# Attention probabilities and the retention output turned by VectorE in 32x32 blocks and through device memory instead of by TensorE

## The chip, the core and the metric

The kernel runs on one core of a Trainium2 chip. TensorE (PE) multiplies, ScalarE (ACT) and VectorE (DVE) do elementwise work, GpSimd (POOL) some small steps, and SyncE (SP) issues most DMAs, which move data between device memory and the core's buffers on 16 DMA engines. The metric is the time of one execution on the device, in microseconds (us); smaller is better.

## What is computed

A decoder of two layers over 256 tokens, width 1024, all in float32. In each layer a mixer of attention (8 heads, three dilated groups) and retention (4 heads), then a gated convolution MLP:

```python
def token_mixer(x, positions, w_in, w_attn_proj, w_ret_proj, ret_gn_g, ret_gn_b, w_out):
    proj = x @ w_in
    attn_qkv, ret_q, ret_k, ret_v, ret_g, gate_a, gate_r = jnp.split(proj, offsets, axis=-1)
    ...
        o, l = dilated_window_attention(attn_qkv[:, :, gi, 0], attn_qkv[:, :, gi, 1], attn_qkv[:, :, gi, 2], window, dilation)
    ...
    ret = chunkwise_retention(...)
    ret = head_group_norm(ret, ret_gn_g, ret_gn_b)
    ret = (jax.nn.silu(ret_g.astype(jnp.float32)) * ret).astype(x.dtype)
    merged = jax.nn.sigmoid(gate_a) * (attn @ w_attn_proj) + jax.nn.sigmoid(gate_r) * (ret @ w_ret_proj)
    return merged @ w_out

def reference(...):
    for i in range(DEPTH):
        mix = token_mixer(...)
        x = layer_norm(DN_ALPHA * x + mix, ln1_g[i], ln1_b[i])
        ple = jax.nn.sigmoid(x @ w_ple_gate[i]) * (p[i] @ w_ple_proj[i])
        x = layer_norm(DN_ALPHA * x + conv_ffn(x, w_up[i], conv_w[i], conv_b[i], w_down[i]) + ple, ln2_g[i], ln2_b[i])
    return x
```

## The kernel before

Weights stream through a ring of three slots in chunks of 1 MB (2048 floats on each of 128 partitions). SP loads a chunk into `raw` once the chunk three before it has been used up by DVE (`load` waits on `lo_ready`). ACT copies it, rounded, to `w_hi` (`to_hi`), DVE takes the difference as `w_lo` (`to_lo`), and PE multiplies with both parts. In chunk c's step ACT and DVE make chunk c + 2. Every engine runs its own program in a fixed order, and semaphores tie them; nothing is scheduled by a planner.

A layer's mixer has four passes (j = 0 to 3) of 15 chunks; pass j makes two attention heads and one retention head. `both_parts` is a chunk of one kind of product (5.6 us on PE), `two_chunks` multiplies two chunks together (chunks 1 and 2, and 11 and 12), `by_token` is chunk 0. The head work stands between the chunks (`behind(c)` on PE): the scores of head 0 behind chunk 9, the retention scores behind 12, the scores of head 1 and the retention products behind 13. DVE masks the scores, takes the maximum, and normalises the probabilities in `prob` (`normalise(0)` in chunk 11's step, `normalise(1)` in chunk 14's), then scales the retention output into `ret_y`. All these live in the tensor `scratch`, the name that the profile shows.

The products with the values need the probabilities with the keys on the partitions, so TensorE transposes them: `transpose_prob` turns the 8 blocks of 128x128 of one head into the banks `acc`, and ACT copies them to `probT` (`copy_probT`). Head 0's stand behind chunk 12, head 1's behind chunk 0 of the next pass, together with the 8 of the retention output (`transpose_ret`), which ACT's `finish_ret` takes with scale and bias to `ret_t`; DVE multiplies by the gate, and both make the parts `ret_hi` and `ret_lo`. `attend` follows behind chunks 1 and 2. After the last pass a merge begins with two gate chunks, the product with `ret` in two halves, attention in between, and the product with `attn`; there the transposes stand behind the gate chunks. In all, 192 transposes: 24 for each of 8 passes.

SP's only work is the DMA queue, in program order: a wait there holds everything behind it.

Of the kernel before, what the change touches and what calls it, by code (L numbers as in the profile page):

```python
# [22 lines left out]
P = 128  # L23
# [9 lines left out]
RV = 512  # L33
# [64 lines left out]
def program(nc, x, xT, positions, w_in, w_attn_proj, w_ret_proj, w_out, w_up, w_down,  # L98
            w_ple_gate, ple_operands, ln_rows, feature_params, constants, out):
    ctx = ExitStack()  # L100
    with ctx:
# [47 lines left out]
        probT = view(0, (2, TT, 512))  # L149
        prob = view(2048, (TT, 512))  # L150
        decayed = view(3456, (384,))
        ret_y = view(3840, (TT, RV))
        silu = view(4864, (4, SEQ))
# [3 lines left out]
        ret_t = view(6912, (4, SEQ))  # L157
        qk = view(7936, (6, 2, SEQ))
# [62 lines left out]
        probT_done, probT_copied, pv_done = sem("probT_done"), sem("probT_copied"), sem("pv_done")  # L221
# [8 lines left out]
        ret_yT_done, ret_affine, ret_gated = sem("ret_yT_done"), sem("ret_affine"), sem("ret_gated")  # L230
# [45 lines left out]
        def _(sp):  # L276
# [20 lines left out]

            def mixer_loads(l, j, c_from):
# [11 lines left out]
                for c in range(c_from, C_MIX):  # L310
                    load(l, l * C_LAYER + j * C_MIX, c, part(w_in, l, 0, KT, cols[c], CH))

# [4 lines left out]
            for l in range(DEPTH):  # L317
# [27 lines left out]
                load(l, g, 1, part(w_in, l, 0, KT, GR0, CH))  # L345
                load(l, g, 2, part(w_ret_proj, l, 0, KT, 0, CH))
                load(l, g, 3, part(w_ret_proj, l, KT, KT, 0, CH))
                load(l, g, 4, part(w_attn_proj, l, 0, KT, 0, CH))
                for j in range(NJ - 2):
# [49 lines left out]
        def _(act):  # L399
# [26 lines left out]
            def copy_probT(a, n):  # L426
                act.wait_ge(probT_done, n)
                for t in range(TT):
                    ins = nc.scalar.activation(probT[:, a, t, :], acc[t][:, :], ACT.Copy)
                ins.then_inc(probT_copied, 1)  # L430

            def finish_ret(l, j, done, src):

                act.wait_ge(ret_yT_done, done)
                act.wait_ge(feat_in, 16 * DEPTH)
                for k in range(4):
                    ins = nc.scalar.activation(ret_t[:, k, :], src[k // 2][:, (k % 2) * SEQ:(k % 2 + 1) * SEQ],
# [3 lines left out]
                if j < NJ - 1:  # L441
                    copy_probT(1, done * 2)
# [20 lines left out]
            def mixer(l, j):  # L463
# [15 lines left out]
                def retention_scores():  # L479
                    copy_probT(0, it2 + 1)  # L480
                    act.wait_ge(decayed_ready, it + 1)
                    nc.scalar.activation(decayed_hi, decayed, ACT.Copy).then_inc(decayed_hi_ready, 1)
# [7 lines left out]
                for c in range(C_MIX):  # L490
# [6 lines left out]
                    if j and c == 1:  # L497
                        finish_ret(l, j - 1, it, (acc[2], acc[3]))
# [15 lines left out]
                    if j and c == 0:  # L514
                        gates_silu(l, j)
                    if c == v0:
# [50 lines left out]
            for l in range(DEPTH):  # L567
# [23 lines left out]
                for c in range(5):  # L591
# [4 lines left out]
                    if c == 1:  # L596
                        finish_ret(l, NJ - 1, (l + 1) * NJ, (acc[2], acc[3]))
                        gate_sigmoid(0, 0)
                        gate_low(c0 + 1, 0, 1)
                    if c == 2:  # L600
                        copy_probT(1, (l + 1) * NJ * 2)
# [165 lines left out]
        def _(dve):  # L767
# [153 lines left out]
            def mixer(l, j):  # L921
# [60 lines left out]

                def decay_scores():
# [21 lines left out]
                for c in range(C_MIX):  # L1005
# [6 lines left out]
                    if j and c == 1:  # L1012
                        finish_ret(j - 1, it)
                    if j and c == 3:
                        finish_attn(j - 1, it)
                    if c in (rv, rv + 1):
# [7 lines left out]
                        else:  # L1024
                            nc.vector.tensor_tensor(rv_lo[:, t, :], bank[bank_of(c)][:, :], rv_hi[:, t, :].bitcast(F32),
                                                    ALU.subtract).then_inc(bank_read[bank_of(c)], 1)
                    if one_by_one and c == 3:
# [12 lines left out]
                    if c == 11:  # L1040
                        normalise(0)
                    if c == 12:
                        decay_scores()
                    if c == 14:
                        normalise(1)
                        dve.wait_ge(gn_rstd, it + 1)
# [3 lines left out]
                                                ALU.subtract, ALU.mult).then_inc(ret_y_ready, 1)  # L1050
                        high_part(14, silu[:, 2:4, :], 1.0)
# [747 lines left out]
```

## Time and profile before

| | before |
|---|---|
| time, median of 3 runs | 1482.85 us (1482.59 to 1483.01) |
| span of the profiled execution | 1480.9 us |
| PE busy | 1471.0 us, 99% |
| DVE busy | 1017.0 us, 69% |
| ACT busy | 784.8 us, 53% |
| DMA | 266.86 MB, mean 180 GB/s |

The profiled execution is one run; its span goes from the first to the last instruction, and the 2.0 us between it and the median lie outside. An engine's timeline row gives the start, the length, the line, the operation and its tensors, and in brackets how long the engine was idle before it and what ended that. In the chain that ended last, followed back from the end, PE has 96%.

### The profile page before, as it was taken

How to read it: one execution, taken by the hardware profiler on the slowest of the kernel's cores; microseconds unless marked ns; L12 is line 12 of the kernel's file. 1: busy time of each engine (PE TensorE's matmuls, PEld its weight loads, DVE VectorE, ACT ScalarE, POOL GpSimd, SP SyncE). 2: the span in 40 equal slices, each digit the busy share in tenths (PEclk: the TensorE clock that was granted, in tenths of full speed). 3: DMA queues.
4: the chain of work that ended last, by engine and by line, in shares of the span. 5: the costliest groups of instructions: out<-in, count | busy, mean ns of one | idle time of the engine just before them, and what ended most of it. 6: DMA issues, size and time to landing. Idle time of an engine off the chain costs nothing.

```text
span 1480.9 us, 20354 instructions
## 1 busy us (share of the span) xinstructions
PE 1471.0 (99%) x8369; PEld 1292.9 (87%) x8369; DVE 1017.0 (69%) x1165; ACT 784.8 (53%) x845; POOL 46.0 (3%) x30
## 2 busy tenths in 40 slices
PE   9999999999999999999999999999999999999998
PEld 8888898888888888888888888888888888888886
DVE  6765665756755688777866657667566556887777
ACT  5564554554744456566544545546446444566562
POOL 0000000000000020000010000000000000100000
PEclk9999999999999999999999999999999999999999
DMA  9745446455456565655555555454545565665560
GB/s 315 236 145 170 155 158 199 143 170 168 147 188 214 181 213 178 207 197 199 175 173 167 168 171 165 150 194 147 170 149 187 177 205 177 202 221 177 181 237 36
DMA packets 232621, 266.86 MB, mean 180 GB/s; under 512 B 4320, under 2 KB 222944, under 8 KB 231904
## 3 DMA queue, kind: packets, MB, share of 16 engines
q1 hardware_dynamic: 231728, 264.96, 53.8%
q8 instruction: 58, 0.95, 0.3%
q10 hardware_dynamic: 816, 0.79, 0.2%
q14 instruction: 19, 0.16, 0.0%
HBM read 264.68 MB, written 1.05 MB: 179 GB/s over the span
## 4 chain that ended last, share of the span: by engine, by line
PE 96%; DMA 1%; DVE 1%; ACT 1%; issue 0%; SPq 0%; DVEq 0%; ACTq 0%
PE bank L1337 39%; PE bank L1342 20%; PE bank L1323 7%; PE bank L1325 6%; PE bank L1324 6%; PE acc L1323 4%; PE acc L1324 4%; PE acc L1325 4%; DMA raw<-w_in 1%; PE acc L1510 1%; PE acc L1487 1%; PE acc L1465 1%; PE acc L1483 1%; PE acc L1472 0%; PE acc L1530 0%; PE acc L1452 0%
## 5 line engine op out<-in xcount | busy, mean ns | idle before, releaser
L775 DVE TENSOR_TENSOR w_lo<-raw,w_hi 128x2048 fp32r<-128x2048 f32 x234 | 535.6, 2289 | 262.8 <-ACT w_hi L408 262.5
L408 ACT ACTIVATE w_hi<-raw 128x2048 fp32r<-128x2048 f32 x241 | 459.5, 1908 | 149.8 <-PE bank L1325 80.1
L1337 PE MATMUL bank<-xT_both,w_hi 128*128 128x512 f32 x2208 | 528.3, 391 | 0.2 <-DVE scratch L932 0.2
L1337 PEld LDWEIGHTS bank<-xT_both,w_hi 128*128 128x128 f32 x2208 | 407.5, 188 | 81.3 <-DVE scratch L932 0.4
L1342 PEld LDWEIGHTS bank<-xT_both,w_lo 128*128 128x128 f32 x2208 | 283.1, 191 | 10.8
L1342 PE MATMUL bank<-xT_both,w_lo 128*128 128x256 f32 x2208 | 286.4, 283 | 0.0
L528 ACT ACTIVATE scratch<-bank 128x512 f32<-128x512 f32 x80 | 47.8, 598 | 229.6 <-PE bank L1342 229.6
L1323 PE MATMUL bank<-w_hi,xT_both 128*128 128x512 f32 (+1 forms) x464 | 162.1, 349 | 0.4 <-DVE xT_both L843 0.3
L1325 PE MATMUL bank<-w_hi,xT_both 128*128 128x512 f32 (+1 forms) x464 | 161.0, 347 | 0.0
L1324 PE MATMUL bank<-w_lo,xT_both 128*128 128x512 f32 (+1 forms) x464 | 160.9, 347 | 0.0
L1185 DVE SCALAR_TENSOR_TENSOR scratch<-scratch,feat 128x256 f32<-128x256 f32 x176 | 77.4, 481 | 33.7 <-ACT scratch L685 28.8
L1323 PEld LDWEIGHTS bank<-w_hi,xT_both 128*128 128x128 f32 x464 | 88.6, 191 | 11.8 <-issue 0.9
L1325 PEld LDWEIGHTS bank<-w_hi,xT_both 128*128 128x128 f32 x464 | 88.6, 191 | 10.8
L1324 PEld LDWEIGHTS bank<-w_lo,xT_both 128*128 128x128 f32 x464 | 88.6, 191 | 10.2
L932 DVE SCALAR_TENSOR_TENSOR scratch<-bank,scratch 128x512 f32<-128x512 f32 x80 | 55.1, 689 | 60.2 <-ACT scratch L528 60.1
L1323 PE MATMUL acc<-w_hi,mid_hi 128*128 128x512 f32 x224 | 87.7, 392 | 0.3 <-DVE mid_lo L794 0.3
L1324 PE MATMUL acc<-w_lo,mid_hi 128*128 128x512 f32 x224 | 87.5, 391 | 0.0
L1325 PE MATMUL acc<-w_hi,mid_lo 128*128 128x512 f32 x224 | 87.2, 389 | 0.0
L678 ACT ACTIVATE scratch<-bank 128x512 f32<-128x512 f32 x42 | 25.1, 597 | 85.7 <-PE bank L1342 85.7
L1337 PE MATMUL bank<-ret,w_hi 128*128 128x512 f32 x256 | 61.4, 392 | 0.0
L1337 PEld LDWEIGHTS bank<-ret,w_hi 128*128 128x128 f32 x256 | 47.0, 188 | 9.1
L1323 PEld LDWEIGHTS acc<-w_hi,mid_hi 128*128 128x128 f32 x224 | 42.1, 188 | 9.2 <-DVE mid_lo L794 1.2
(173 smaller groups left out, 1385.5 us busy)
## 6 DMA issues: line engine op xcount, KB each, us to landing
raw<-w_in SPq DMA_DIRECT2D x133, 1024.0 KB, 5.0
raw<-w_up SPq DMA_DIRECT2D x44, 1024.0 KB, 5.1
raw<-w_down SPq DMA_DIRECT2D x20, 1024.0 KB, 5.1
raw<-w_ret_proj SPq DMA_DIRECT2D x16, 1024.0 KB, 5.1
raw<-w_attn_proj SPq DMA_DIRECT2D x8, 1024.0 KB, 5.1
raw<-w_out SPq DMA_DIRECT2D x8, 1024.0 KB, 5.1
raw<-w_ple_gate SPq DMA_DIRECT2D x8, 1024.0 KB, 5.1
scratch<-ln_rows SPq DMA_DIRECT2D x4, 1024.0 KB, 7.2
```

What stands on the lines that cost most here:

```text
L408: nc.scalar.activation(w_hi[:, s, :], raw[:, s, :], ACT.Copy).then_inc(hi_ready, 1)
L528: nc.scalar.activation(dst, pair[pair_of(c)][:, :, SEQ:2 * SEQ], ACT.Copy, scale=ATT_SCALE if c in (3, 5, 7) else 1.0).then_inc(mix_low, 1)
L678: nc.scalar.activation(hpad[:, 2 * half:2 * half + 2, 2:2 + SEQ], pair[half][:, :, SEQ:2 * SEQ], ACT.Copy).then_inc(up_low, 1)
L775: nc.vector.tensor_tensor(w_lo[:, s, :], raw[:, s, :], w_hi[:, s, :].bitcast(F32), ALU.subtract).then_inc(lo_ready, 1)
L932: nc.vector.scalar_tensor_tensor(out=dst, in0=pair[pair_of(c)][:, :, 0:SEQ], scalar=scale, in1=dst, op0=ALU.mult, op1=ALU.add).then_inc(ba ...
L1185: ins = nc.vector.scalar_tensor_tensor(out=conv[:, 2 * half + b, :], in0=hpad[:, 2 * half + b, tap:tap + SEQ], scalar=feat[:, l, bass.ds(i ...
L1323: mm(dst, st_hi, mv_hi, start=start, stop=False)
L1324: mm(dst, st_hi, mv_lo, start=False, stop=False)
L1325: return mm(dst, st_lo, mv_hi, start=False, stop=stop)
L1337: mm(pair[p][:, m, :], hi[:, o:o + P], src[:, k0 + k, :, :].rearrange("p a t -> p (a t)"), start=first and k == 0, stop=False)
L1342: ins = mm(pair[p][:, m, SEQ:2 * SEQ], lo[:, o:o + P], src[:, k0 + k, 0, :], start=False, stop=last and k == KT - 1)
L1465: ins = nc.tensor.transpose(acc[t][:, o * P:(o + 1) * P], prob[:, t, o * P:(o + 1) * P], ident)
```

## The change

Each head's probabilities, and the retention output, are turned in two steps. DVE transposes every 32x32 block within itself (one `transpose` of 128x1024 for each of the three). SP then writes the result to device memory (`blocks_out`, rows of 128 floats) and reads it back with the blocks in their transposed places (`blocks_in`, four DMAs of 32 partitions, each row of 32 floats, 128 bytes). TensorE's transposes and ACT's copies are gone. `attend` waits for the reads (`probT_in`), head by head; `finish_ret` on ACT waits for `ret_yT_in` and stands behind the copy of the rv bank. On SP the new DMAs stand behind the weight loads 1, 2 and 4 of the next pass (or of the merge).

```diff
+            def blocks_out(dst, src, written):
+
+                sp.dma_start(dst.rearrange("b p k -> p b k"), src.rearrange("p (b k) -> p b k", k=P)).then_inc(written, 16)
+
+            def blocks_in(dst, src, landed):
+
+                for n in range(4):
+                    v = slice(n * 32, (n + 1) * 32)
+                    sp.dma_start(dst[v, :].rearrange("p (b r) -> p b r", r=32),
+                                 src[:, :, v].rearrange("b (i p) r -> p (b i) r", p=32)).then_inc(landed, 16)
...
+            def turned_blocks(it, c):
+
+                if c == 1:
+                    prob_out(0, it)
+                if c == 2:
+                    prob_in(0, it)
+                if c == 4:
+                    prob_out(1, it)
+                    ret_out(it)
+                    prob_in(1, it)
+                    ret_in(it)
...
-                act.wait_ge(ret_yT_done, done)
+                act.wait_ge(ret_yT_in, 64 * done)
...
-                    if j and c == 1:
-                        finish_ret(l, j - 1, it, (acc[2], acc[3]))
...
+                    if j and c == 1:
+                        finish_ret(l, j - 1, it)
                     if c == v0:
...
+                def turn_prob(a):
+
+                    dve.wait_ge(prob_ready, it2 + a + 1)
+                    nc.vector.transpose(prob_flat[a], prob.rearrange("p t k -> p (t k)")).then_inc(prob_turned, 1)
+
+                def turn_ret():
+
+                    dve.wait_ge(ret_y_ready, it + 1)
+                    nc.vector.transpose(ret_t_flat, ret_y_flat).then_inc(ret_turned, 1)
...
                     if c == 14:
                         normalise(1)
+                        turn_prob(1)
...
+                        turn_ret()
                         high_part(14, silu[:, 2:4, :], 1.0)
...
             def attend(done):
-                pe.wait_ge(probT_copied, done * 2)
                 for a in range(2):
+                    pe.wait_ge(probT_in[a], 64 * done)
...
-                    if j and c == 0:
-                        transpose_ret(it, (acc[2], acc[3]))
-                        transpose_prob(it2)
                     if j and c == 2:
                         attend(it)
...
                         ins.then_inc(ret_scores_done, 1)
-                        transpose_prob(it2 + 1)
```

The order on VectorE from the w_lo of chunk 1 (made in chunk 14's step) to the one of chunk 3, before; the line of `to_lo` is L775, of the high part of a chunk L932, of `finish_ret` L906 and L908:

```order
L775 TENSOR_TENSOR w_lo<-raw,w_hi 128x2048
L977 RECIPROCAL stat<-stat 128x2
L980 TENSOR_SCALAR scratch<-scratch,stat 128x512 x2
L1047 TENSOR_SCALAR scratch<-acc,stat 128x512
L1049 TENSOR_SCALAR scratch<-acc,stat 128x512
L932 SCALAR_TENSOR_TENSOR scratch<-bank,scratch 128x512
L775 TENSOR_TENSOR w_lo<-raw,w_hi 128x2048 x2
L906 TENSOR_TENSOR scratch<-scratch 128x1024
L908 TENSOR_TENSOR ret<-scratch,ret 128x4x256
L1025 TENSOR_TENSOR mid_lo<-bank,mid_hi 128x512
```

and the same place on VectorE now, where L819 is `to_lo`, L976 the high part, L950 and L952 `finish_ret`:

```order
L819 TENSOR_TENSOR w_lo<-raw,w_hi 128x2048
L1021 RECIPROCAL stat<-stat 128x2
L1024 TENSOR_SCALAR scratch<-scratch,stat 128x512 x2
L1030 STREAM_TRANSPOSE scratch<-scratch 128x1024
L1103 TENSOR_SCALAR scratch<-acc,stat 128x512
L1105 TENSOR_SCALAR scratch<-acc,stat 128x512
L1035 STREAM_TRANSPOSE scratch<-scratch 128x1024
L976 SCALAR_TENSOR_TENSOR scratch<-bank,scratch 128x512
L819 TENSOR_TENSOR w_lo<-raw,w_hi 128x2048 x2
L1077 TENSOR_TENSOR mid_lo<-bank,mid_hi 128x512
L950 TENSOR_TENSOR scratch<-scratch 128x1024
L952 TENSOR_TENSOR ret<-scratch,ret 128x4x256
```

Two transposes stand ahead of the high part that frees chunk 14's bank and ahead of the w_lo of chunk 2, and `finish_ret` has moved behind the rv part.

On SyncE's queue now, from the first loads of the second pass; L294 is a weight load, L310 a block write, L316 block reads (before, this is an unbroken run of L284 loads):

```order
L294 DMA raw<-w_in 128x8x256 x2
L310 DMA prob_blocks<-scratch 128x8x128
L294 DMA raw<-w_in 128x8x256
L316 DMA scratch<-prob_blocks 32x32x32 x4
L294 DMA raw<-w_in 128x8x256 x2
L310 DMA prob_blocks<-scratch 128x8x128
L310 DMA ret_blocks<-scratch 128x8x128
L316 DMA scratch<-prob_blocks 32x32x32 x4
L316 DMA scratch<-ret_blocks 32x32x32 x4
L294 DMA raw<-w_in 128x8x256 x12
```

The load of chunk 5 stands behind two writes and eight reads.

## Rows read from the trace of the kernel before

**Rows 1.** The page: the span, and TensorE's busy time.

```profile
span 1480.9 us, 20354 instructions
PE 1471.0 (99%) x8369; PEld 1292.9 (87%) x8369; DVE 1017.0 (69%) x1165; ACT 784.8 (53%) x845; POOL 46.0 (3%) x30
```

**Rows 2.** What PE waited for: us in total, times, longest.

```profile
PE bank L1426 <- DVE stat L851: 1.6, 1, 1.6
```

**Rows 3.** PE's groups by form: count, busy us, mean ns of one, idle before.

```profile
L1465 PE MATMUL acc<-const,scratch 128*128 128x128 f32 x128 | 16.6, 273 | 0.0
...
L1472 PE MATMUL acc<-const,scratch 128*128 128x128 f32 x64 | 8.3, 273 | 0.0
```

**Rows 4.** PE's timeline at a seam: end of chunk 12, start of chunks 1 and 4.

```profile
273.81 1.02 PE L1530 MATMUL acc<-scratch 128*128 128x256 f32 x4
...
298.28 0.48 PE L1323 MATMUL bank<-w_hi,xT_both 128*128 128x512 f32 x1
...
317.95 3.82 PE L1337 MATMUL bank<-xT_both,w_hi 128*128 128x512 f32 x16
```

**Rows 5.** The chain of waits in order of time: start, us, what.

```profile
275.28 0.87 PE acc L1465 x8
...
296.77 0.87 PE acc L1472 x8
297.65 0.87 PE acc L1465 x8
```

**Rows 6.** DVE's timeline at the same seam, the last row at the merge.

```profile
276.02 2.29 DVE L775 TENSOR_TENSOR w_lo<-raw,w_hi 128x2048 fp32r<-128x2048 f32 x1 [4.64 <-ACT w_hi L408]
...
281.24 2.29 DVE L775 TENSOR_TENSOR w_lo<-raw,w_hi 128x2048 fp32r<-128x2048 f32 x1 [1.25 <-ACT w_hi L408]
...
288.38 2.29 DVE L775 TENSOR_TENSOR w_lo<-raw,w_hi 128x2048 fp32r<-128x2048 f32 x1
...
290.77 0.88 DVE L980 TENSOR_SCALAR scratch<-scratch,stat 128x512 f32<-128x512 f32 x2
...
293.01 0.68 DVE L932 SCALAR_TENSOR_TENSOR scratch<-bank,scratch 128x512 f32<-128x512 f32 x1
293.61 2.28 DVE L775 TENSOR_TENSOR w_lo<-raw,w_hi 128x2048 fp32r<-128x2048 f32 x1
...
301.45 1.22 DVE L906 TENSOR_TENSOR scratch<-scratch 128x1024 f32<-128x1024 f32 x1
...
388.98 0.68 DVE L932 SCALAR_TENSOR_TENSOR scratch<-bank,scratch 128x512 f32<-128x512 f32 x1
```

**Rows 7.** ACT's timeline at the seam: `finish_ret`'s steps and two w_hi.

```profile
299.11 1.92 ACT L437 ACTIVATE scratch<-acc,feat 128x256 f32<-128x256 f32 x4
...
302.71 1.06 ACT L444 ACTIVATE ret<-scratch 128x1024 fp32r<-128x1024 f32 x1 [0.70 <-DVE scratch L906]
...
309.54 1.91 ACT L408 ACTIVATE w_hi<-raw 128x2048 fp32r<-128x2048 f32 x1 [4.91 <-PE bank L1325]
...
311.83 1.91 ACT L408 ACTIVATE w_hi<-raw 128x2048 fp32r<-128x2048 f32 x1
```

**Rows 8.** PE's timeline at the merge: second gate chunk, ret product, attention, second half.

```profile
393.18 3.90 PE L1337 MATMUL bank<-xT_both,w_hi 128*128 128x512 f32 x16
...
399.62 3.90 PE L1337 MATMUL bank<-ret,w_hi 128*128 128x512 f32 x16
...
405.27 0.81 PE L1483 MATMUL acc<-scratch 128*128 128x256 f32 x4
...
408.29 3.90 PE L1337 MATMUL bank<-ret,w_hi 128*128 128x512 f32 x16
```

**Rows 9.** SP's timeline at the merge: one load's issue.

```profile
386.66 0.37 SPq L284 DMA_DIRECT2D raw<-w_attn_proj  x1
```

**Rows 10.** The page's DMA issues: count, KB each, median us to landing.

```profile
raw<-w_in SPq DMA_DIRECT2D x133, 1024.0 KB, 5.0
...
out<-X SPq DMA_DIRECT2D x4, 256.0 KB, 2.0
```

**Rows 11.** Two stretches, mixer and MLP: last columns PE clock, DMA share, GB/s.

```profile
130.00:370.00 240.00, 240.00 (x1385) 212.36 (x1384) 154.42 (x176) 120.52 (x132) 5.50 (x2) 1.00 0.51 166
1320.00:1460.00 140.00, 140.00 (x768) 122.21 (x767) 111.45 (x132) 85.50 (x97) 0.00 (x0) 1.00 0.53 180
```

More of the change, by code:

```diff
@@ L149, in program @@
         probT = view(0, (2, TT, 512))
+        prob_flat = [view(a * TT * 512, (TT * 512,)) for a in range(2)]
         prob = view(2048, (TT, 512))
@@ L220, in program @@
         exp_done, inv_ready, prob_ready = sem("exp_done"), sem("inv_ready"), sem("prob_ready")
-        probT_done, probT_copied, pv_done = sem("probT_done"), sem("probT_copied"), sem("pv_done")
+        prob_turned, pv_done = sem("prob_turned"), sem("pv_done")
+        prob_written = [sem(f"prob_written{a}") for a in range(2)]
+        probT_in = [sem(f"probT_in{a}") for a in range(2)]
+        ret_turned, ret_written, ret_yT_in = sem("ret_turned"), sem("ret_written"), sem("ret_yT_in")
         attn_hi_ready, attn_lo_ready = sem("attn_hi_ready"), sem("attn_lo_ready")
@@ L424, in x_high, with finish_ret @@
                                          ACT.Copy).then_inc(xT_hi_ready, 1)
[L426 to L432, printed above, removed]
-                act.wait_ge(ret_yT_done, done)
+            def finish_ret(l, j, done):
+                act.wait_ge(ret_yT_in, 64 * done)
                 act.wait_ge(feat_in, 16 * DEPTH)
                 for k in range(4):
-                    ins = nc.scalar.activation(ret_t[:, k, :], src[k // 2][:, (k % 2) * SEQ:(k % 2 + 1) * SEQ],
+                    ins = nc.scalar.activation(ret_t[:, k, :].rearrange("p (t q) -> p t q", t=TT), ret_yT[:, :, k, :],
                                                ACT.Identity, scale=feat[:, l, j * 4 + PC_GG + k:j * 4 + PC_GG + k + 1],
@@ L596, in _ @@
                     if c == 1:
-                        finish_ret(l, NJ - 1, (l + 1) * NJ, (acc[2], acc[3]))
                         gate_sigmoid(0, 0)
                         gate_low(c0 + 1, 0, 1)
+                        finish_ret(l, NJ - 1, (l + 1) * NJ)
                     if c == 2:
-                        copy_probT(1, (l + 1) * NJ * 2)
                         act.wait_ge(ret_lo_ready, (l + 1) * NJ)
@@ L1026, in mixer @@
                                                     ALU.subtract).then_inc(bank_read[bank_of(c)], 1)
+                    if j and c == 1:
+                        finish_ret(j - 1, it)
                     if one_by_one and c == 3:
@@ L1459, in transpose_x @@
                     transpose_half(n + 1, t, h)
-            def transpose_prob(n):
-                pe.wait_ge(prob_ready, n)
-                for t in range(TT):
-                    for o in range(4):
-                        ins = nc.tensor.transpose(acc[t][:, o * P:(o + 1) * P], prob[:, t, o * P:(o + 1) * P], ident)
-                ins.then_inc(probT_done, 1)
-            def transpose_ret(done, dst):
-                pe.wait_ge(ret_y_ready, done)
-                for t in range(TT):
-                    for k in range(4):
-                        ins = nc.tensor.transpose(dst[k // 2][:, (k % 2) * SEQ + t * P:(k % 2) * SEQ + (t + 1) * P],
-                                                  ret_y[:, t, k * P:(k + 1) * P], ident)
-                ins.then_inc(ret_yT_done, 1)
             def attend(done):
-                pe.wait_ge(probT_copied, done * 2)
                 for a in range(2):
+                    pe.wait_ge(probT_in[a], 64 * done)
                     d = slice(a * P, (a + 1) * P)
```

40 lines of the change are left out of this document (28 added, 12 removed).

## The prediction

> **What bounds the kernel now.** I read the page of engines first: PE is busy 1471.0 of 1480.9 us, DVE 69%, ACT 53% [rows 1]. The list of what PE waited for is next, and there is next to nothing in it: five lines, the first 1.6 us in all [rows 2]. So TensorE's own work sets the time, and whatever leaves it is a gain unless something else comes late in its place. The transposes that go are in the lines' own views: 128 at L1465 and 64 at L1472 [rows 3]. After that only one kind of place matters, since all the transposes stand at the seams between two passes of the mixer (and between the last pass and the merge): the timelines of PE, DVE, ACT and SP there, of one seam near 298 us and of the merge near 392 us [rows 4 to 9].
>
> **What goes from TensorE.** Eight transposes hold PE 0.87 us in the chain of waits [rows 5]. A pass had 24, so 2.61 us, and eight passes 20.9 us. That is the most the change can give: 1482.85 - 20.9 = 1462.0 us. ACT also loses four copies of 128x512 a pass; it waits for PE all the same, 4.91 us before one w_hi [rows 7], so that is worth nothing by itself.
>
> **What comes to VectorE, and where.** Three transposes of 128x1024 f32 a pass. The first stands after normalise(0), where DVE next sat idle for 4.64 us until the w_hi at 276.02 [rows 6]: free. The other two stand in chunk 14's step. There DVE works without a gap from the w_lo at 281.24 to the w_lo at 293.61, which ends at 295.89 [rows 6]; the stretch hangs, through ACT's w_hi that released the row at 276.02, on the end of PE's chunks 11 and 12, not on what PE does after them. The last w_lo is that of chunk 2 of the next pass, and PE's two-chunk matmul of chunks 1 and 2 waits for it. PE started that matmul at 298.28 [rows 4], 2.4 us after the w_lo was done. All 24 transposes lie between the end of chunk 12 (273.81) and this start, so PE will ask for it at 298.28 - 2.61 = 295.67. DVE will have it at 295.89 plus two transposes.
>
> The trace shows no transpose on DVE. The nearest rows: a 128x1024 f32 operation with two inputs takes 1.22 us (L906); two scalar operations of 512 take 0.88 us together (L980) [rows 6]. Bounds: 0.9 us, and twice the first, 2.4 us. I take 1.22, the rate of most f32 rows (0.68 us for 512 elements at L932, 2.28 for 2048 at L775). Then w_lo is ready at 298.33 and PE starts at about 298.4: **0.1 us later than before**. At six of the eight seams (three in each layer) the 2.61 us are gone, because DVE's chain takes the place of PE's. That is 6 x 0.1 = 0.6 us against us.
>
> At the two merges the order is kinder. The second gate chunk began at 393.18 [rows 8]; without 16 transposes PE asks for it at 391.44, and the bank it needs is freed by DVE's high part of chunk 14, at 388.98 + 0.68 = 389.66 before [rows 6], now at 392.1. From there gate, half of the retention product and attention follow at their old lengths [rows 8] (6.44 less 0.87 of transposes, 5.65 and 3.02 us) to 406.3, where the second half of the retention product began at 408.29: up to 1.9 us gained at each, if its operand is there.
>
> **What comes to the DMA queue.** Each pass writes three blocks of 512 KB in packets of 512 B and reads them back in packets of 128 B, in twelve DMAs. On SP they stand between weight loads: the first pair behind loads 1 and 2 of the next pass, where SP waits for w_lo anyway and nobody needs the result for 25 us; the other two behind load 4. On the time axis of the 298 us seam: load 4 goes out when the w_lo of 288.38 ends, at 290.67 [rows 6] (at the merge SP's issue is at 386.66, the same place [rows 9]) and lands 5.0 us later [rows 10], at 295.7. The probabilities are turned at 290.77 + 0.88 + 1.22 = 292.9, the retention output at 292.9 + 1.6 + 1.2 = 295.7. Writes: 256 KB to memory took 2.0 us [rows 10]; behind load 4 I put the landings at 298.0 and 299.8. SP then issues eight reads. One issue takes 0.37 us in the short rows [rows 9], so until about 302.
>
> The price of a packet of 128 B is what decides, and no row has one. The mixer (packets of 1 KB) moved 166 GB/s at a DMA share of 0.51: 0.51 x 16 / 166 = 0.0492 ns a byte, 50 ns a packet. The MLP, a third of whose bytes come in packets of 4 KB, has 0.53 at 180: 0.0471 [rows 11]. So 4 KB packets cost 0.0429 ns a byte, 176 ns each. A straight line through the two sizes has 8 ns fixed and 0.041 ns a byte: 14 ns for 128 B. Bounds: by bytes alone 6 ns; not less than a 1 KB packet, 50 ns. I take **20 ns**: nearer the line, since four times the size moved the price per byte by only 13%, but above it, since the line is stretched by a factor of eight. The two blocks are 8192 packets, 512 on each DMA engine, and 1.8 of a load's 5.0 us are not its data (1 MB at 0.0492 ns a byte on 16 engines is 3.2), with 0.3 for SP's step: the retention output lands at s = 298.0 + 2.1 + 0.512 X (X in ns), 310.3 at 20, 307.3 at 14, 325.7 at 50, and near 304 (SP's issues) at 6.
>
> One statement of the Trainium skill (DMA: Bandwidth & Descriptors, "Why small descriptors are slow") speaks for cheap packets: it gives a packet about three cycles beside one for each 32 B. By it my estimate would be 7 cycles of its 850 MHz, 8 ns, and the sum that of the cheap rival below, 1480 instead of 1500 us; no row here shows a packet of that size.
>
> **Who waits for the landing.** ACT does, at finish_ret, which now stands behind the rv copy of chunk 1, with its to_hi(4), the other rv copy and everything later queued behind it. From s: four affine steps 1.92, the product on DVE 1.22, ret_hi 1.06, w_hi 1.91, w_lo 2.29, rv_lo as L932 0.68 [rows 6, 7], with hops 9.3 us until PE may start chunk 4 (its weights and bank 1). PE started chunk 4 at 317.95 [rows 4] and will ask at 318.05. So the landing is hidden up to s = 308.75, which is X = 17 ns. At 20 ns chunk 4 starts at 319.6, **1.55 us late**, at six seams. At the merge the chain is affine, product, ret_hi and ret_lo (as the product): s + 5.7. On the seam's axis the old start is 312.32 (408.29 less the 95.97 us between the two seams' rows of L932 [rows 6]); at 20 ns it is 316.0, **3.7 us late**, twice. Attention stands one chunk (5.65 us) and its own 3.02 us ahead of chunk 4, at 309.3, and at the merge at 307.4; the second probability block, read first, lands at 305.2, hidden up to X = 28. Load 5 is issued at 302 in place of 296 and lands near 314, its w_hi stood at 311.83 and moves behind finish_ret to 317: hidden.
>
> **Sum.** 6 x (0.1 + 1.55) + 2 x 3.7 = 17.3 us more. The span of the profiled execution, 1480.9, becomes 1498.2; what lies outside the span, 1482.85 - 1480.9 = 2.0 us, stays: 1500.2 us. Nothing else on TensorE moves.
>
> **Rivals.**
> Cheap packets (up to 16 ns): the reads come back before anyone needs them. Then the mixer seams give 0.1 us of loss each and the merges run from +0.7 (14 ns) to -1.9 (8 ns or less): 1484.9 down to 1479.7; with a DVE transpose of 0.9 us the seams gain 0.54 each as well, 1476. For it: the line through the two sizes. Against: no row lies below 1 KB. This is the one that ends not slower; it decides at X = 17 ns, or at 15 ns for the time as a whole to stay inside 0.2%.
> Dear packets (above 30 ns): at 30, s = 315.5 and 6 x 6.85 + 2 x 8.9 = 59 us more, 1542; at 35, 1562; at 50, with s = 325.7, 141 us more, 1624. For it: descriptors of a fixed price, and reads that hop over memory. Against: the line.
> Dear transposes, cheap packets: at 2.4 us for a DVE transpose each mixer seam ends 2.36 us later, 14 us in all, and the merges 2.4 each more: 1504. For it: data crossing partitions may not stream like an addition. Against: the f32 rows of 512, 1024 and 2048 elements all run near 1.1 to 1.3 ns an element.
> The Trainium skill (VectorE: DVE Perf Modes, "The three transpose paths") gives 311 ns for a 128x128 transpose in 16 bits, by my estimate 2.5 us for 1024 columns, which would be this rival; no row here has the operation, and part of the 311 ns may be start-up.
>
> **Chances.** Forecast (packets of 17 to 30 ns, transposes near 1.2 us) 0.40; cheap packets 0.29; dear packets 0.17; dear transposes with cheap packets 0.12; anything else 0.02. A measurement of this kernel tells about 0.2% (3 us) from nothing. Faster by more than that takes packets under about 9 ns or a transpose under 1.1 us beside cheap ones: 0.11. Within 0.2% is the rest of the cheap case: 0.19. Slower: 0.70. The range reaches from 1478 to 1562 us (35 ns a packet), which leaves out the dearest packets and the double luck below.
>
> **What would show each step.** In the profile after: (1) PE's matmuls fall by 192, and its busy time by about 21 us. (2) A new row in PE's waits: the matmul at the start of chunk 1 waits for DVE's w_lo, near 2.7 us at six seams; if DVE's transpose rows say 1.2 us, this step is right. (3) The median landing of the 32-row reads, and ACT's wait at the affine step for the DMA: some 6 us at each seam at 20 ns. If ACT doesn't wait there, packets were cheap. (4) PE's wait at chunk 4 and, at the merge, at the matmul that reads the second half of ret. What would break the sum: writes to memory that confirm much later than 2 us, an issue on SP that takes longer for the many short rows than 0.37 us, or a granted clock that falls after PE's new gaps (1.00 in both stretches of [rows 11], where PE never stops).

## The result, and the profile after

| | before | after |
|---|---|---|
| time, median (lowest to highest) | 1482.93 us (1482.59 to 1483.51), 4 runs | 1494.93 us (1494.51 to 1495.06), 4 runs |
| ratio after / before | | 1.0078, 95% interval 1.0066 to 1.0090 |
| span of the profiled execution | 1480.9 us | 1493.3 us |

The change makes the kernel 0.8% slower. The forecast was 1500.2 us, 5.3 us above the time, and the range holds it. The sum behind it holds less well, as the sections below show: its largest term did not occur, and an effect that it left out is nearly as large.

The page of the kernel after: engines, DMA packets and two groups of issues (KB each, median us to landing). It answers to [rows 1] and [rows 10].

```profile
PE 1460.3 (98%) x8177; PEld 1278.8 (86%) x8177; DVE 1047.4 (70%) x1189; ACT 768.7 (51%) x813; POOL 45.9 (3%) x30
...
DMA packets 357420, 292.00 MB, mean 196 GB/s; under 512 B 104544, under 2 KB 347744, under 8 KB 356704
...
prob_blocks<-scratch SPq DMA_DIRECT2D x16, 512.0 KB, 4.3
scratch<-prob_blocks SPq DMA_DIRECT2D x64, 128.0 KB, 4.2
```

TensorE has its 192 matmuls less (8369 to 8177), and yet only 10.7 of the 20.9 us have left its busy time. Its idle time, span less busy, went from 9.9 to 33.0 us. What it waited for says where most of that is (us in total, times, longest):

```profile
PE bank L1380 <- DVE w_lo L819: 15.9, 6, 2.7
PE bank L1394 <- DVE ret L952: 5.2, 2, 2.8
PE bank L1394 <- DVE scratch L976: 2.2, 3, 1.1
```

The first two are new: six mixer seams and two merges. The third is the high part of a chunk, for which the kernel before waited 0.2 us in all: 0.55 us at each merge, and 1.1 at the kernel's start, long before the first exchange. Together 23.3 us of waiting stand against 20.9 us of transposes. The rest of the loss is not in the list of waits at all. It is in the granted clock. Seven stretches of the kernel after, each just behind one of the eight gaps of the first two lines; behind the one left out, at 107 us, the clock was 1.00 too (length; busy time of the engines; last columns clock, DMA share, GB/s):

```profile
200.00:210.00 10.00, 7.36 (x29) 5.89 (x28) 5.71 (x4) 3.34 (x3) 0.00 (x0) 0.83 1.20 209
300.00:310.00 10.00, 8.60 (x38) 7.15 (x39) 4.24 (x3) 3.19 (x5) 0.00 (x0) 1.00 1.25 186
410.00:420.00 10.00, 7.83 (x35) 6.60 (x36) 6.47 (x5) 5.87 (x7) 0.00 (x0) 0.83 0.53 181
840.00:850.00 10.00, 7.35 (x41) 6.47 (x40) 8.56 (x7) 5.10 (x5) 0.00 (x0) 0.84 1.05 264
940.00:950.00 10.00, 7.35 (x32) 6.03 (x31) 6.38 (x5) 3.34 (x3) 0.00 (x0) 0.83 1.22 220
1040.00:1050.00 10.00, 7.89 (x35) 6.57 (x36) 4.95 (x3) 3.74 (x4) 0.00 (x0) 1.00 1.10 164
1150.00:1160.00 10.00, 7.16 (x32) 5.91 (x32) 7.46 (x6) 5.75 (x6) 0.00 (x0) 0.83 0.46 163
```

A mean of 0.83 over 10 us is 3.4 us at half speed, and the rows of PE's timeline in the first of these stretches show it directly (start, length):

```profile
203.56 0.47 PE L1380 MATMUL bank<-w_hi,xT_both 128*128 128x512 f32 x1 [2.64 <-DVE w_lo L819]
...
204.79 0.42 PE L1382 MATMUL bank<-w_hi,xT_both 128*128 128x512 f32 x1
205.03 0.61 PE L1380 MATMUL bank<-w_hi,xT_both 128*128 128x512 f32 x1
205.44 0.63 PE L1381 MATMUL bank<-w_lo,xT_both 128*128 128x512 f32 x1
...
208.42 0.41 PE L1382 MATMUL bank<-w_hi,xT_both 128*128 128x512 f32 x1
```

PE stands still for 2.64 us, runs for 1.5 us at 2.4 GHz, a matmul starting every 0.23 us, then at 1.2 GHz, one every 0.42 us, until 208.42, and then at 2.4 GHz again. Eight matmuls start between 205.03 and 208.42, in 3.4 us where they need 1.8: 1.6 us are lost. Such a stretch at 1.2 GHz is called a fall below. The five of them cost 8.0 us.

**Ledger of the span, 1480.9 to 1493.3 us, 12.4 us.** Five falls of the clock: 8.0. The rest can be read from when PE starts the same matmul in both kernels. Before, that of chunks 1 and 2 was at these times in passes 2 and 3 (and at 298.28 in pass 4 [rows 4]):

```profile
106.34 0.48 PE L1323 MATMUL bank<-w_hi,xT_both 128*128 128x512 f32 x1
...
202.31 0.48 PE L1323 MATMUL bank<-w_hi,xT_both 128*128 128x512 f32 x1
```

After, it is at 107.33, 203.56 and 301.40. From the first to the second of these seams PE lost 0.26 us. From the second to the third it lost 1.87, of which 1.6 is the fall at 205, so the third seam's own share is near 0.26 again. Six times 0.26 is 1.6 us. The first seam stands 0.99 late, 0.7 more than a seam's own share. These 0.7 us are older than any exchange. They come at the kernel's start, where ACT and DVE still wait for the first weights to land, before and after:

```profile
35.52 2.79 PE L1337 MATMUL bank<-xT_both,w_hi 128*128 128x512 f32 x11 [0.21 <-DVE scratch L932]
```

```profile
36.23 2.11 PE L1394 MATMUL bank<-xT_both,w_hi 128*128 128x512 f32 x8 [1.11 <-DVE scratch L976]
```

Two kernels below that are the kernel before up to that place, the first of the experiments and the one with DVE's transposes alone, have this wait with 1.2 and 0.9 us, so it is not the exchange's; why it is 0.2 in the kernel before is open. The merges are 0.8 and 1.3 us late, from rows shown below. Sum 8.0 + 1.6 + 0.7 + 2.0 (0.77 + 1.26) = 12.3 us.

### The profile page after: what moved, and what is told of

Read it like the earlier page. It is cut to its first block, busy times and chain, and to the rows that moved or that the text cites. A ratio compares the mean times of both kernels' runs of the same rounds, so it can differ in the third digit from the quotient of the medians.

```text
span 1493.3 us, 20079 instructions
## 1 busy us (share of the span) xinstructions
PE 1460.3 (98%) x8177; PEld 1278.8 (86%) x8177; DVE 1047.4 (70%) x1189; ACT 768.7 (51%) x813; POOL 45.9 (3%) x30
## 4 chain that ended last, share of the span: by engine, by line
PE 80%; DVE 11%; ACT 3%; DMA 3%; SPq 1%; issue 1%; DVEq 0%; ACTq 0%
PE bank L1394 34%; PE bank L1399 17%; PE bank L1380 6%; PE bank L1381 6%; PE bank L1382 6%; DVE w_lo L819 5%; PE acc L1380 3%; PE acc L1381 3%; PE acc L1382 3%; ACT w_hi L462 2%; DMA raw<-w_in 1%; SPq L316 1%; PE acc L1529 1%; DVE scratch L1030 1%; DVE stat L1015 1%
## 5 line engine op out<-in xcount | busy, mean ns | idle before, releaser
L819 DVE TENSOR_TENSOR w_lo<-raw,w_hi 128x2048 fp32r<-128x2048 f32 x234 | 535.4, 2289 | 201.7 <-ACT w_hi L462 201.3
L1399 PEld LDWEIGHTS bank<-xT_both,w_lo 128*128 128x128 f32 x2208 | 283.1, 191 | 10.7
L1380 PE MATMUL bank<-w_hi,xT_both 128*128 128x512 f32 (+1 forms) x464 | 164.2, 354 | 16.3 <-DVE w_lo L819 15.9
L1382 PE MATMUL bank<-w_hi,xT_both 128*128 128x512 f32 (+1 forms) x464 | 162.8, 351 | 0.0
L976 DVE SCALAR_TENSOR_TENSOR scratch<-bank,scratch 128x512 f32<-128x512 f32 x80 | 54.8, 686 | 55.4 <-ACT scratch L573 55.3
L1394 PE MATMUL bank<-ret,w_hi 128*128 128x512 f32 x256 | 64.5, 407 | 5.2 <-DVE ret L952 5.2
```

The source lines that it names most:

```text
L819: nc.vector.tensor_tensor(w_lo[:, s, :], raw[:, s, :], w_hi[:, s, :].bitcast(F32), ALU.subtract).then_inc(lo_ready, 1)
L976: nc.vector.scalar_tensor_tensor(out=dst, in0=pair[pair_of(c)][:, :, 0:SEQ], scalar=scale, in1=dst, op0=ALU.mult, op1=ALU.add).then_inc(ba ...
L1380: mm(dst, st_hi, mv_hi, start=start, stop=False)
L1382: return mm(dst, st_lo, mv_hi, start=False, stop=stop)
L1394: mm(pair[p][:, m, :], hi[:, o:o + P], src[:, k0 + k, :, :].rearrange("p a t -> p (a t)"), start=first and k == 0, stop=False)
L1399: ins = mm(pair[p][:, m, SEQ:2 * SEQ], lo[:, o:o + P], src[:, k0 + k, 0, :], start=False, stop=last and k == KT - 1)
```

## The experiments

Times are medians. The kernel before, run again beside each of them on the same chip, had medians of 1482.9 to 1483.1 us; the ratios are to those.

**What the transposes are worth by themselves.** The kernel before with two transposes for each group of eight; the probabilities and the retention output are left untransposed for the rest.

```diff
-                    for o in range(4):
-                        ins = nc.tensor.transpose(acc[t][:, o * P:(o + 1) * P], prob[:, t, o * P:(o + 1) * P], ident)
+                    ins = nc.tensor.transpose(acc[t][:, 0:P], prob[:, t, 0:P], ident)
```

> The kernel before with two transposes in each group in place of eight; the other 144 are left out, so the probabilities and the retention output are mostly not turned. Theory A (TensorE's own work sets the time and VectorE has 2.4 us of slack at each seam): 18 x 0.109 = 1.96 us less in each of 8 passes, below the slack, so 15.7 us less: 1467.2 us. Rival (another chain of the seam is as long as TensorE's already): much of it doesn't come, above 1475 us.

Measured 1469.61 us (1469.27 to 1469.93), ratio 0.9909 (0.9893 to 0.9926): 13.3 us gained for 144 transposes, where 15.7 us at 0.109 us each were due, so 85% of it. Most of the rest stands at two places of its trace: the kernel's start, 0.6 us, and the attention of the merges, where PE waits 1.3 us in two gaps for ACT's copy of the probabilities. The price of a transpose from [rows 5] is right and the gain is to be had, if nothing new comes late.

**Is it the gap that makes the clock fall?** After, with 16 identity transposes put on PE in front of the late matmul. They compute nothing that is read.

```diff
+            def fill(n):
+                pe.wait_ge(scores_masked, n)
+                for t in range(TT):
+                    for o in range(4):
+                        for _ in range(2):
+                            nc.tensor.transpose(acc[t][:, o * P:(o + 1) * P], const[:, CC_ID:CC_ID + P], ident)
...
+                    if j and c == 0:
+                        fill(it2)
```

> The changed kernel with 16 transposes of the identity on TensorE behind chunk 0 of each pass but the first of a layer; nobody reads them. They need 1.74 us and stand in the gap of 2.65 us that TensorE spends waiting for VectorE's w_lo. Theory A (the gap is VectorE's chain, and the low clock that follows three of the six gaps comes from the gap): the work costs nothing, gaps shrink to 0.9 us, the three stretches at half clock at the seams go, 1.7 us each: 1489.8 us with a mean clock near 0.997. Rival (the clock falls for another reason): the time stays at 1494.9 us and the clock at 0.993. Rival (the gap is not idle for TensorE): 6 x 1.7 us more, 1505 us.

Measured 1492.20 us (1488.28 to 1492.58), ratio 1.0054 (1.0037 to 1.0071), 2.7 us less than after. What PE waited for in this kernel, and two stretches of it:

```profile
PE bank L1394 <- DVE ret L952: 5.9, 2, 3.3
PE bank L1380 <- DVE w_lo L819: 5.4, 6, 0.9
```

```profile
1147.00:1157.00 10.00, 7.68 (x28) 6.36 (x29) 6.47 (x5) 5.70 (x6) 0.00 (x0) 0.66 0.40 131
...
200.00:210.00 10.00, 9.11 (x53) 7.80 (x52) 5.80 (x4) 3.93 (x4) 0.00 (x0) 1.00 1.11 206
```

Useless work on TensorE makes the kernel faster: the six gaps shrink from 2.65 to 0.9 us, and no seam has a fall any more. The time was expected near 1490 and is 2 us above, because the merges, which were not filled, still fall, and the second of them for longer: 0.66 over 10 us is 6.8 us at 1.2 GHz, where it was 3.4. The gap there is 3.3 us, and the fall begins within it. So the gap is the cause at the seams, since nothing else was changed there. Matmul against matmul with the kernel after, each of the three seams without its fall brings 1.6 us, 4.8 in all, and the second merge takes 1.5 back. One of the four executions had a mean clock of 0.998, where the others had 0.995 and 0.996; it is the one of 1488.28 us.

**What DVE's transposes cost the seam.** After, with each of DVE's transposes cut to 32 of its 1024 columns. The rest of the block is not transposed (set once to zero), and all DMAs stay. This one setting of 128x2048 takes DVE 1.8 us in the first pass and makes PE wait 1.5 us there.

```diff
-                    nc.vector.transpose(prob_flat[a], prob.rearrange("p t k -> p (t k)")).then_inc(prob_turned, 1)
+                    nc.vector.transpose(prob_flat[a][:, 0:32], prob.rearrange("p t k -> p (t k)")[:, 0:32]).then_inc(prob_turned, 1)
```

> The changed kernel, but each VectorE transpose covers 32 columns of 1024, so the rest of the blocks is not turned; all block writes and reads and all waits stay. Theory A (VectorE's two transposes are what the seam pays): w_lo comes about 2.3 us earlier at six seams, gaps fall to about 0.4 us and the low clock there goes; the two merges keep their wait for the retention output: near 1472 us. Rival B (the block transfers and ACT's wait for them are what costs): the time stays above 1487 us.

Measured 1485.39 us (1483.93 to 1487.31), ratio 1.0018 (1.0009 to 1.0028): 9.5 us less than after, but 13 above what was expected; 1.5 of these are the setting to zero. The waits of PE, and ACT's timeline at the seam near 300 us:

```profile
PE bank L1395 <- DVE ret L952: 7.2, 2, 3.9
PE bank L1381 <- DVE w_lo L819: 3.5, 6, 0.6
...
PE bank L1395 <- DVE mid_lo L1077: 2.4, 4, 0.8
```

```profile
307.57 2.08 ACT L485 ACTIVATE scratch<-scratch,feat 128x256 f32<-128x256 f32 x4 [4.75 <-DMA scratch<-ret_blocks]
```

The seams' wait falls from 15.9 to 3.5 us, as it should. Behind it stands what the expectation had left out: with PE 2 us earlier, the landing of the retention output is the next thing that is late. PE waits up to 3.9 us at a merge, and 0.8 at chunk 4 (`mid_lo` L1077) at four seams. One of the gaps, 3.92 us, has a fall behind it that costs 2.9 us in the first 16 matmuls (6.73 us where 3.82 is usual [rows 4]):

```profile
1141.00 6.73 PE L1395 MATMUL bank<-ret,w_hi 128*128 128x512 f32 x16 [3.92 <-DVE ret L952]
```

**What the small packets cost.** After, with each block read back untransposed in one DMA of rows of 512 B. The 32x32 blocks stay in their old places, so what comes back is not the transpose.

```diff
-                for n in range(4):
-                    v = slice(n * 32, (n + 1) * 32)
-                    sp.dma_start(dst[v, :].rearrange("p (b r) -> p b r", r=32),
-                                 src[:, :, v].rearrange("b (i p) r -> p (b i) r", p=32)).then_inc(landed, 16)
+                sp.dma_start(dst.rearrange("p (b k) -> p b k", k=P), src.rearrange("b p k -> p b k")).then_inc(landed, 64)
```

> The changed kernel, but each block is read back as it was written, in one DMA with rows of 512 bytes (1024 packets in place of 4096), so the blocks are not put in their transposed places. VectorE's transposes stay. Theory A (the seams pay for VectorE, the merges for the return of the retention output): the six gaps at the seams stay at 2.65 us, the waits of 2.3 and 2.8 us at the two merges and the low clock behind them go: about 8 us less than 1494.9, 1487 us. Rival (reads are cheap and cost nothing): 1494.9 us.

Measured 1487.57 us (1486.98 to 1489.40), ratio 1.0029 (1.0019 to 1.0040), as expected. PE's waits:

```profile
PE bank L1377 <- DVE w_lo L816: 15.9, 6, 2.6
...
PE bank L1391 <- DVE ret L949: 1.0, 1, 1.0
```

The packets of 128 B touch only the merges (5.2 to 1.0 us of wait); the seams' wait is as in the kernel after. DVE's cost and the DMA's are thus two things at two places. The falls of the clock are elsewhere, though. This trace, of the slowest of the eight executions, has four, all at seams and none at a merge. One is where the kernel after had none behind the same gap of 2.65 us:

```profile
300.00:310.00 10.00, 8.79 (x32) 7.15 (x33) 4.04 (x3) 3.68 (x5) 0.00 (x0) 0.83 0.93 281
```

**Both together.** The cuts of the last two in one kernel.

> The changed kernel with both cuts: VectorE turns only 32 of 1024 columns, and the blocks are read back straight in rows of 512 bytes. With the short transposes alone 1485.4 us was measured, far from the 1472 that the seams alone would give; theory A now says that the return of the retention output took over there as the next bound (finish_ret ahead of chunk 4's work) and cost about 7 us at the merges. Without it: six seams gain 2.0 us each, the merges 1.9 each: 1469 us. Rival (the writes and their waits on SP, which are still here, are what holds it): above 1478 us.

Measured 1472.20 us (1471.22 to 1472.98), ratio 0.9927 (0.9911 to 0.9944).

```profile
PE bank L1378 <- DVE w_lo L816: 3.5, 6, 0.6
...
PE bank L1392 <- DVE ret L949: 0.8, 2, 0.5
```

One cut alone gave 9.5 us, the other 7.4, both 22.7: 5.8 us more than their sum, because the first cut alone runs into the landing that the second removes. PE's longest new wait, 1.5 us, is that behind the setting to zero, and the mean clock is back at 0.999. The time is 3 us above the expected 1469; the setting and the kernel's start (0.9 us) are most of that. With cheap DVE work and cheap packets the exchange would have gained 0.7%.

**What DVE's transposes cost without the exchange.** The kernel before, with two transposes of 128x1024 added on DVE in chunk 14's step, where the change has them; nobody reads them, and TensorE keeps its own.

```diff
+                        dve.wait_ge(prob_ready, it2 + 2)
+                        nc.vector.transpose(qk[:, 0:2, :, :].rearrange("p a b t -> p (a b t)"), prob.rearrange("p t k -> p (t k)"))
+                        dve.wait_ge(ret_y_ready, it + 1)
+                        nc.vector.transpose(qk[:, 2:4, :, :].rearrange("p a b t -> p (a b t)"), ret_y.rearrange("p t k -> p (t k)"))
```

> The kernel before, with TensorE's transposes and no block transfers, plus VectorE's two transposes of 128x1024 in chunk 14's step, with results that nobody reads. Theory A: VectorE's slack at a seam is 2.4 us and the two take 2.45, so the gap that opens on TensorE is 0.2 to 0.3 us, six times: 1484.6 us, with no low clock. Rival (VectorE's place has more slack than read): 1483.0. Rival (VectorE delays other things as well): above 1487.

Measured 1485.01 us (1484.77 to 1485.77), ratio 1.0013 (1.0004 to 1.0023). DVE works 19 us more, and the time moves by 2.1 us. PE's list of waits has one line that has grown, the high part at the kernel's start (0.9 us). At the seam near 298 us PE stands still for 0.2 us, since eight transposes hold it 0.87 us [rows 5]:

```profile
298.15 1.04 PE L1469 MATMUL acc<-const,scratch 128*128 128x128 f32 x8
299.21 0.47 PE L1327 MATMUL bank<-w_hi,xT_both 128*128 128x512 f32 x1
```

At the three seams of the first layer the matmul of chunks 1 and 2 starts at 106.81, 203.01 and 299.21 us, 0.23 more late each time against the kernel before. Six seams make 1.4 us of the 2.1, as theory A has it; 0.2 are from the start, and some tenths come at the attention of the merges.

This is the step of the prediction on DVE's chain seen from the other side. While PE still does its transposes, they cover 2.4 us of what DVE adds; take them away and the same 2.5 us of DVE work stand open. The 2.6 us that TensorE saves at a seam and the 2.5 that VectorE adds there are one for one.

**One head alone.** The kernel before with only head 0's probabilities by DVE and DMA; its transpose stands where DVE was idle.

```diff
+                def turn_prob():
+                    dve.wait_ge(prob_ready, it2 + 1)
+                    nc.vector.transpose(prob_flat, prob.rearrange("p t k -> p (t k)")).then_inc(prob_turned, 1)
...
-                        transpose_prob(it2 + 1)
-                        pe.wait_ge(probT_copied, it2 + 1)
+                        pe.wait_ge(scores_masked, it2 + 1)
```

> The kernel before with only the first head's probabilities turned by VectorE and device memory, where VectorE and the DMA queue have slack; the second head's and the retention output stay on TensorE. Theory A: 8 transposes less in each of 8 passes, 0.87 us each, nothing waits: 1482.9 - 7.0 = 1475.9 us. Rival (the block writes and reads delay weight loads enough to be seen): no gain, 1481 us or more.

Measured 1476.35 us (1476.10 to 1476.99), ratio 0.9954 (0.9938 to 0.9971): 6.6 of the 7.0 us that 64 transposes hold. That part of the change is good, and "free" for the transpose after `normalise(0)` was right.

**The change with its steps where there is slack.** After, with head 1's and the retention's transposes on DVE moved behind the w_lo of chunk 0's step in the next pass, their writes behind load 5 and their reads behind load 6, attention behind chunk 3, `finish_ret` into chunk 3's step. At the merges, where no slack is, head 1 and the retention output go by TensorE as before, so 32 transposes stay. Everything is computed.

```diff
-                    if j and c == 1:
-                        finish_ret(j - 1, it)
-                        turn_prob(1)
-                        turn_ret()
+                    if j and c == 0:
+                        turn_prob(1)
+                        turn_ret()
...
+                    if j and c == 3:
+                        finish_ret(j - 1, it)
```

> A full version, aimed at both bounds: the second head's probabilities and the retention output are turned behind the w_lo of chunk 2 of the next pass, their writes stand behind load 5 and their reads behind load 6, finish_ret and attention come one to two chunks later; at the two merges these two stay on TensorE. Theory A: TensorE asks for w_lo 0.2 us before it is there, so six seams give 2.4 us each, the merges 0.9 each, the first pass nothing for its first group: 1467 to 1468 us. Rival (the transfers slow weight loads, or the later attention runs into something): 1473 us or more.

Measured 1486.23 us (1483.56 to 1488.31), ratio 1.0023 (1.0012 to 1.0033): missed by 19 us. PE's waits, and ACT's timeline near 316 us:

```profile
PE bank L1419 <- DVE scratch L999: 6.6, 7, 2.0
PE acc L1555 <- ACT scratch L507: 5.0, 2, 2.5
```

```profile
316.67 2.08 ACT L507 ACTIVATE scratch<-scratch,feat 128x256 f32<-128x256 f32 x4 [4.74 <-DMA scratch<-ret_blocks]
```

The seam's wait is gone. But the blocks come later as well, so ACT stands 4.74 us at `finish_ret` (30.2 us at six seams), DVE behind it, and the high part that frees a bank (L999) behind DVE. At the merges `finish_ret` stands behind a gate's copy and PE waits for it. This trace is of the fastest of eight executions, 1483.56 us at a mean clock of 0.998; the others had 0.996 to 0.998, so part of the median's 2.7 us above it is the clock.

**The same with `finish_ret` later still.** In chunk 5's step on ACT and DVE; at the merges, ahead of the gate's copies on both.

```diff
-                    if j and c == 3:
+                    if j and c == 5:
...
+                        finish_ret(l, NJ - 1, (l + 1) * NJ)
                         gate_sigmoid(0, 0)
                         gate_low(c0 + 1, 0, 1)
-                        finish_ret(l, NJ - 1, (l + 1) * NJ)
```

> The full version again with two places mended that its trace showed: ACT waited some 5 us for the retention output inside chunk 3's step and TensorE 6.6 us behind it, so finish_ret now stands in chunk 5's step; and at the merges TensorE's second group of transposes waited 2.5 us, twice, for finish_ret, which stands ahead of the gate's copy again. Theory A (nothing is left but the w_lo of chunk 2 and the first pass): 11 us less than 1486.2, 1470 to 1475 us. Rival (more of the transfers' cost is spread over weight loads): 1480 us or more.

Measured **1471.01 us** (1470.54 to 1471.86), ratio **0.9917** (0.9900 to 0.9933), faster than both kernels, with every output computed.

```profile
PE acc L1569 <- DMA scratch<-prob_blocks: 2.3, 2, 1.8
...
PE bank L1419 <- DVE scratch L999: 0.8, 1, 0.8
```

A few lines in other places move 15 us: the high part's 6.6 us of wait are down to the 0.8 at the kernel's start, the 5.0 us at the merges are gone, and the mean clock is 0.999. The exchange moves 160 transposes off PE, 17.4 us by [rows 5], and 11.9 of them arrive in the time.

## Why the prediction was right, and where it was not

**Bound and gain.** Right. TensorE sets the time, the transposes are worth what the chain says, and 13.3 us of it were had with 144 transposes left out, 11.9 with everything computed.

**DVE's transpose.** 1.22 us was taken between 0.9 and 2.4; DVE's groups by form say, of 16 of the 24:

```profile
L1030 DVE STREAM_TRANSPOSE scratch<-scratch 128x1024 f32<-128x1024 f32 x16 | 19.9, 1245 | 0.6
```

The rival of dear transposes falls. So does the estimate of 2.5 us that the prediction made from the Trainium skill (VectorE: DVE Perf Modes, "The three transpose paths"): 1.245 us is half of it.

**The seams.** Right in mechanism, and in size but for 0.16 us a seam. DVE's and PE's timelines at the seam of [rows 4] and [rows 6]:

```profile
294.55 1.25 DVE L1030 STREAM_TRANSPOSE scratch<-scratch 128x1024 f32<-128x1024 f32 x1
...
297.24 1.25 DVE L1035 STREAM_TRANSPOSE scratch<-scratch 128x1024 f32<-128x1024 f32 x1
298.41 0.65 DVE L976 SCALAR_TENSOR_TENSOR scratch<-bank,scratch 128x512 f32<-128x512 f32 x1
298.99 2.27 DVE L819 TENSOR_TENSOR w_lo<-raw,w_hi 128x2048 fp32r<-128x2048 f32 x1
```

```profile
301.40 0.47 PE L1380 MATMUL bank<-w_hi,xT_both 128*128 128x512 f32 x1 [2.65 <-DVE w_lo L819]
```

PE waits 2.65 us for the w_lo that the prediction named, six times, where it expected 2.7. The loss is 0.26 us a seam in place of 0.1, 1.0 us in all. With TensorE's transposes left in, DVE's two cost 0.23 us a seam, which is the same step without the DMAs.

**Chunk 4, 1.55 us late six times: did not occur.** This was 9.3 us, the largest term. PE has no wait at chunk 4 in the list above. SP and ACT at the same seam:

```profile
300.14 2.57 SPq L316 DMA_DIRECT2D scratch<-prob_blocks  x4
302.76 3.41 SPq L316 DMA_DIRECT2D scratch<-ret_blocks  x4
```

```profile
309.85 2.08 ACT L485 ACTIVATE scratch<-scratch,feat 128x256 f32<-128x256 f32 x4 [2.09 <-DMA scratch<-ret_blocks]
```

The whole program stands 3.02 us later here than the prediction's axis (301.40 against 298.38), so s was 309.85 - 3.02 = 306.8, not 310.3. It is below the 308.75 from which chunk 4 would have been late. ACT waited for the landing all the same, 18.6 us at the eight places together, where the prediction's third sign had some 6 us at each seam. The chain behind s was right: in the kernel with short transposes, ACT's row is at 307.57 while PE's matmul of chunks 1 and 2 starts at 296.47, which puts s at 307.57 + 1.91 = 309.5 on the same axis, 0.7 past the point, and PE waited up to 0.8 us at chunk 4.

What failed is the step from a packet's price to the landing. As the length of a packet, 20 ns was well taken. In the stretch from 130 to 370 us:

```profile
130.00:370.00 240.00, 234.71 (x1328) 206.74 (x1327) 162.66 (x181) 116.48 (x124) 5.50 (x2) 0.99 0.68 192
```

the share rose by 0.17 over [rows 11], that is 0.17 x 240 x 16 = 653 us of engine time, for the 30720 packets that two passes add. Less 25 us for each thousand of the 6144 packets of 512 B (0.0492 ns a byte, as in the prediction), that leaves 20 ns for one of 128 B. Packet by packet the trace has a mean of 17.7 ns for one of 128 B and 27.6 for one of 512 B. But in the stretches with the block reads the share reads 1.20 and 1.25, more than 16 engines can be busy one packet at a time. The packets' times overlap, so 512 packets an engine pass in less than 512 times their length. The trace has it directly: the 8192 packets of the two blocks begin between 301.22 and 308.49 us, which is 7.27 us for 512 an engine, 14.2 ns each, and ACT starts 1.4 us after the last. 14 ns is what the prediction's line through two sizes gave, before it was raised to 20, and s at 14 is 307.3 by the prediction's own sum, against 306.8 measured. The 8 ns of its paragraph on fixed cycles are too few. SP's issue of a read was under-priced too: 0.64 and 0.85 us each, not 0.37, so the last read was out at 306.17, 303.2 on that axis, not 302. It hid behind the landing: the last packet began 2.3 us after it. The first write was confirmed by 297.1 (300.14 - 3.02), where 298.0 was taken.

**The merges, 3.7 us late twice: 0.8 and 1.3.** The same step. PE's timeline at the first merge, beside [rows 8], and at the second, and ACT's row at the first:

```profile
395.35 3.93 PE L1394 MATMUL bank<-xT_both,w_hi 128*128 128x512 f32 x16 [0.55 <-DVE scratch L976]
...
412.18 4.21 PE L1394 MATMUL bank<-ret,w_hi 128*128 128x512 f32 x11 [2.32 <-DVE ret L952]
...
1153.38 2.06 PE L1394 MATMUL bank<-ret,w_hi 128*128 128x512 f32 x5 [2.84 <-DVE ret L952]
```

```profile
406.44 2.08 ACT L485 ACTIVATE scratch<-scratch,feat 128x256 f32<-128x256 f32 x4 [4.62 <-DMA scratch<-ret_blocks]
```

On the seam's axis this is 406.44 - 95.97 - 3.12 = 307.35. The prediction's s + 5.7 gives 313.05, 0.73 after 312.32; measured, 412.18 - 408.29 - 3.12 = 0.77. The gap of 2.32 us is this delay and the time that the transposes left. The second merge is 0.5 us worse: 1153.38 against 1142.61 before, less the 9.51 by which the last seam stood late already (1042.11 against 1032.60), is 1.26. Its reads were issued no later, but ACT's row ended its wait at 1147.65, 0.5 us later beside PE's work than at the first.

**The clock: not in the sum.** The prediction names it as what would break it, after PE's new gaps, and that is what came, 8.0 us. No row of before could size it, since PE has no such gap there. It should have been a rival with a range.

**So the forecast came near because two misses cancel.** Out of the sum go 9.3 us at chunk 4 and 5.4 at the merges; in come 8.0 of the clock, 1.0 at the seams and 0.7 at the kernel's start. 17.3 - 14.7 + 9.7 = 12.3, the measured change of the span but for rounding. What took place at the seams and merges is nearly the rival of cheap packets, 1484.9 us at 14 ns, plus the falls of the clock. That the time lies within 5.3 us of the forecast is luck.

## What to carry to other kernels

- Taking work off the bounding engine pays only as far as the next engine's chain leaves room at that place: count the slack there against what the other engine gets. Here 2.6 us were freed and 2.5 added in the same gap; moved to where there was slack, and left on TensorE at the merges, the exchange gained 0.8%.
- Several things become due at one seam. Relieve one and read which is next before expecting the gain.
- A new gap of 2 to 3 us on an otherwise full TensorE can cost another 1.6 us behind it; look at the granted clock behind it, and price it as a term.

## What the runs showed of the hardware

- **Clock.** In the kernel after, five of eight gaps of 2.3 to 2.8 us were followed by 3.4 us at 1.2 GHz, which cost 1.6 us each, and three were not, of the same length and at like places of the program. In the kernel with straight reads the six seams had the same gaps of 2.65 us, and the falls were behind four of them, the first and the third among these, which had none in the kernel after. A gap of 3.9 us (short transposes) and one of 3.3 (filled seams) went with 6.8 us at 1.2 GHz that began within the gap, and another of 3.3 (short transposes) with none. Gaps of 0.9 us and less at the seams had none in any run. The length of the gap alone doesn't decide it, nor does the place; what else does is open.
- **VectorE** transposes 128x1024 f32 in 32x32 blocks in 1.245 us; the product of two such tensors takes 1.22.
- **DMA.** A write of 512 KB in rows of 512 B landed 4.3 us after issue (median of the probabilities' writes; the row of 256 KB in [rows 10] had 2.0), a read of 128 KB in rows of 128 B after 4.2. Packets of 128 B took 17.7 ns each on average and passed at one in 14.2 ns an engine. SP took 0.64 and 0.85 us to issue such a read at the seam near 300 us, against 0.37 for a load of 1 MB [rows 9].
